# A branch hint for the back edge of the loop over pairs of expert jobs, on TensorE, ScalarE and VectorE

## The reference

```python
def swiglu(h, wg, wu, wd):
    return (jax.nn.silu(h @ wg) * (h @ wu)) @ wd

def moe_swiglu(h, router_w, wg, wu, wd):
    logits = (h @ router_w).astype(jnp.float32)
    top_val, top_idx = lax.top_k(logits, TOP_K)          # TOP_K = 2
    top_w = jax.nn.softmax(top_val, axis=-1)
    gates = jnp.sum(jax.nn.one_hot(top_idx, N_EXPERTS) * top_w[..., None], axis=-2)
    y = jnp.zeros_like(h)
    for e in range(N_EXPERTS):                            # 8 experts, 1024 x 3584 each
        y = y + gates[..., e:e + 1] * swiglu(h, wg[e], wu[e], wd[e])
    return y
```

## Time and profile before

| | us |
|---|---|
| median of 3 runs | 1384.22 (1383.19 to 1384.24) |
| span of the profiled execution | 1382.1 |
| jobs 0 and 1 end, loop entered (TensorE) | 759 |
| back edge (TensorE) | 960 to 967 |
| exit (TensorE) | 1169 to 1173 |

### The profile page before, as it was taken

How to read it: one execution, slowest core, us unless ns; L and a number is a source line. 1 busy time by engine, 2 the same in 40 slices (tenths; PEclk the granted TensorE clock), 3 DMA queues, 4 the chain that set the end, 5 groups by cost and what they waited for, 6 DMA issues and landing times.

```text
span 1382.1 us, 17732 instructions
## 1 busy us (share of the span) xinstructions
PE 1368.8 (99%) x6681; PEld 938.3 (68%) x6681; DVE 808.3 (58%) x1143; ACT 661.5 (48%) x886; POOL 10.3 (1%) x22
## 2 busy tenths in 40 slices
PE   8999999999999999999999999999999999999998
PEld 7887788888898877843434888534888534888532
DVE  5878666554557786631113989423889423989311
ACT  7657646444366575511002787312787302787210
POOL 2000000000000000000000000000000000000000
PEclk9999999999999999999999999999999999999999
DMA  9555446555544576899999999999999999999997
GB/s 354 191 177 184 152 136 231 183 183 184 182 153 155 181 264 269 309 403 429 429 433 427 430 431 428 429 432 428 429 430 423 399 431 427 430 429 430 428 430 295
DMA packets 84242, 454.90 MB, mean 329 GB/s; under 512 B 5624, under 2 KB 7936, under 8 KB 58048
## 3 DMA queue, kind: packets, MB, share of 16 engines
q1 hardware_dynamic: 83232, 452.47, 81.7%
q0 software_dynamic: 752, 1.23, 0.3%
q10 hardware_dynamic: 176, 0.07, 0.0%
HBM read 452.69 MB, written 1.06 MB: 328 GB/s over the span
## 4 chain that ended last, share of the span: by engine, by line
PE 92%; DVE 3%; ACT 3%; DMA 2%; issue 1%; DVEq 0%; ACTq 0%; SPq 0%
PE pA L837 39%; PE pB L837 19%; PE pB L1351 10%; PE pA L1351 8%; PE pA L1415 7%; PE pA L861 2%; DMA first_run<-expert_w_gate_dram 2%; PE pB L861 1%; DVE w_lo L1873 1%; PE pB L1249 1%; ACT w_hi L1514 1%; PE pA L1279 0%; PE pB L1069 0%; ACT early_hi L1514 0%; DMA aqk<-mix_norm_g_dram 0%
## 5 line engine op out<-in xcount | busy, mean ns | idle before, releaser
L1873 DVE TENSOR_TENSOR w_lo<-raw,w_hi 128x1024 fp32r<-128x1024 f32 x128 | 153.1, 1220 | 58.0 <-ACT w_hi L1514 57.6
L1873 DVE TENSOR_TENSOR w_lo<-first_run,w_hi 128x1024 fp32r<-128x1024 f32 x126 | 149.1, 1219 | 30.9 <-ACT w_hi L1514 29.6
L1514 ACT ACTIVATE w_hi<-raw 128x1024 fp32r<-128x1024 f32 x128 | 131.9, 1058 | 56.2 <-PE pB L837 32.2
L1873 DVE TENSOR_TENSOR w_lo<-late,w_hi 128x1024 fp32r<-128x1024 f32 x126 | 150.8, 1222 | 11.9 <-ACT w_hi L1514 3.6
L1514 ACT ACTIVATE w_hi<-first_run 128x1024 fp32r<-128x1024 f32 x126 | 130.9, 1065 | 52.0 <-DMA first_run<-expert_w_gate_dram 26.5
L1514 ACT ACTIVATE w_hi<-late 128x1024 fp32r<-128x1024 f32 x126 | 131.8, 1060 | 30.6 <-PE pA L837 15.1
L1824 ACT ACTIVATE ex_act<-pA 64x512 f32<-64x512 f32 x15 | 8.9, 591 | 242.0 <-PE pA L1351 194.4
L1873 DVE TENSOR_TENSOR early_lo<-raw,early_hi 128x1024 fp32r<-128x1024 f32 x58 | 69.8, 1221 | 34.3 <-ACT early_hi L1514 34.2
L2373 DVE TENSOR_TENSOR x<-pA,x 128x512 f32<-128x512 f32 x28 | 18.8, 688 | 118.2 <-PE pA L1280 116.9
L1351 PE MATMUL pB<-late,x_narrow 128*64 128x512 f32 x272 | 78.0, 592 | 0.0
L837 PE MATMUL pA<-w_hi,hT_hi 128*128 128x512 f32 x192 | 77.1, 402 | 0.0
(11 more groups left out here) (463 smaller groups left out, 2792.8 us busy)
## 6 DMA issues: line engine op xcount, KB each, us to landing
first_run<-expert_w_gate_dram SPq DMA_DIRECT2D x28, 1792.0 KB, 17.7
first_run<-expert_w_up_dram SPq DMA_DIRECT2D x28, 1792.0 KB, 15.3
late<-expert_w_gate_dram SPq DMA_DIRECT2D x28, 1792.0 KB, 15.5
late<-expert_w_up_dram SPq DMA_DIRECT2D x28, 1792.0 KB, 17.4
raw<-w_in_dram SPq DMA_DIRECT2D x43, 1024.0 KB, 5.1
first_run<-expert_w_down_dram SPq DMA_DIRECT2D x21, 2048.0 KB, 15.9
late<-expert_w_down_dram SPq DMA_DIRECT2D x28, 1024.0 KB, 17.6
late<-expert_w_down_dram SPq DMA_DIRECT2D x14, 2048.0 KB, 21.9
```

The lines of the kernel that those rows point to most:

```text
L1514: f(like_raw(m, halves_slot(m)[0]), raw_slot(m), ACT.Copy).then_inc(s["w_hi_done"], 1)
L1873: tt(like_raw(m, lo), raw_slot(m), like_raw(m, hi.bitcast(F32)), ALU.subtract).then_inc(s["w_lo_done"], 1)
```

## The change

`nc.Fori` with one engine stands in the place of the engine's own `Fori`, with the same bounds and the same body. With `hint_back_edge=True` one more instruction is put at the head of the body: a branch prefetch hint that names the compare-and-branch at the body's end and says that it will be taken. It runs in each round. Nothing else in the program differs; SyncE and GpSimd have no such loop.

```diff
@@ -1481,7 +1481,7 @@
             rounds = load_pair_count(pe)
-            with pe.Fori(0, rounds) as i:
+            with nc.Fori(0, rounds, engines=[pe.engine], hint_back_edge=True) as i:
                 job(2 * i + 2, i)
                 narrow_job(i + 2, 2 * i + 3, "wide", "wide", i + 1)
@@ -1842,7 +1842,7 @@
             rounds = load_pair_count(eng)
-            with eng.Fori(0, rounds) as i:
+            with nc.Fori(0, rounds, engines=[eng.engine], hint_back_edge=True) as i:
                 job(2 * i + 2, i)
                 narrow_job(i + 2, 2 * i + 3, "wide", "wide", i + 1)
```

## The result

The changed kernel takes 1390.88 us (median; 1389.90 to 1392.29), the kernel before 1384.22 on the same chip: a ratio of 1.0054, 95% interval 1.0044 to 1.0065, so 0.4% to 0.65% slower. (The ratio is worked out from the single runs; the quotient of the two medians is 1.0048.) Forecast were 1391.8 us, as rival A. The total fits. Its terms are another matter: two of them were wrong and cancelled.

A forecast was written before the change was run, and what follows sets the result against it. TensorE and the loads were taken as full in the expert stage, so only delays to TensorE count. Terms -3.5 + 3.5 + 7.6 = +7.6 on a 1382.1 us span, with 2.1 around it, give 1391.8 us; range 1380.6 to 1397.0.

The forecast's parts named there:

- rival A: The forecast itself: wrong hint at the exit, exposed on ScalarE and VectorE, 1391.8 us (1387 to 1398); chance 0.44.
- Part 1: Loop heads: three hint instructions, run twice each, cost 0; 0.5 us more if nothing covered them.
- Part 2: TensorE's back edge: head's block fetched early removes pause and low clock; between 0 and -3.68, taken as -3.5 us.
- The 1.54 us for the clock: Behind TensorE's back-edge pause: granted clock at 0.50 from 967.2 to 970.6 us costs 1.54 of the 3.68 us.
- Part 3, TensorE: At the loop exit: the wrong hint leaves the next block unfetched, stopping TensorE as at the back edge, +3.5 us.
- Rival B: The wait only moves from TensorE's back edge to its exit, other engines unaffected: 1384.2 us; chance 0.20.
- Part 3, ScalarE and VectorE: Behind the exit: wrong hints stop both engines, 2.2 us of TensorE pause plus low clock each, 3.8 each, +7.6 us.
- The stop S: Behind the exit: ScalarE or VectorE waits some 5.3 us for its code, costing TensorE S - 3.1.
- the cover of 3.1 us: Behind the exit: slack 1.7 us from four slots, plus 1.36 us until the next piece is due, hides that much stop.
- The remark on SiLU in the bounds: Upper bound behind the exit, 15.0 us if no slack is left: at SiLU (L1803) ScalarE has little.
- Rival C: Back edge mended, exit free because prefetch turns to the next block after the branch falls through: 1381.0 us; chance 0.24.
- Rival D: The hint changes nothing, prefetch being purely sequential: 1384.2 us, up to 1384.7; chance 0.12.

The follow-up runs named there:

- slot 0: Against the kernel before, TensorE's loop head at a fetch block's start: ratio 0.9998 without hint, 0.9993 with constant hint, 0.9979 with register hint (not taken in last round).
- 76 or 128: Against the kernel before, TensorE's loop alone with register hint, head at instruction 76 or 128 of its fetch block: 1382.53 us (0.9992) and 1382.49 us (0.9993).
- slot 46: Against the kernel before, TensorE's loop alone with register hint, head at instruction 46 of its fetch block: 1383.67 us, ratio 1.0003.
- VectorE alone: Against the kernel before, the constant hint on VectorE's loop only: 1386.87 us, ratio 1.0028.
- ScalarE alone: Against the kernel before, the constant hint on ScalarE's loop only: 1387.86 us, ratio 1.0030.

## Why the prediction was right, and where it was not

**Part 1**, the hints themselves at 0: right as far as the runs tell. Their rows are 31 to 61 ns, a register move in their place leaves the time as it was, and so do true hints on ScalarE and VectorE.

**Part 2**, TensorE's back edge at -3.5 us: wrong. The step "if the head's block is fetched before the branch needs it" was granted, not weighed. The bound "0 (the fetch comes no earlier)" was named, and it is what happened: branch 6270 ns. With the head at slot 0, 76 or 128 the hint mends it (266 to 510 ns), at slot 46, 2 us behind a boundary, it doesn't. That the changed kernel's branch is also close behind one is the reading that fits (it takes 5944 and 6270 ns in two profiles, no less than without a hint, and the register-move run has the two packets there); the place itself was not measured. The 1.54 us for the clock, of the 3.68, are also not there in every execution. Of ten profiled pauses of 2.0 to 2.7 us, five were followed by a granted clock of 0.50 (before, VectorE alone, ScalarE alone behind the exit, slot 0 with the constant hint, slot 46) and five were not. The kernel before happened to be profiled with one. Its 104 single runs beside the experiments fit that: in 71 the mean granted clock was 0.999 (median 1382.99 us), in 33 it was 0.997 or 0.998 (median 1384.11). So the low clock is worth some 1.1 us in a third of the executions, not 1.54 in all, and the 1384.22 us that the forecast started from looks to be of the longer kind.

**Part 3, TensorE**, +3.5 at the exit: wrong, and it cancelled part 2. The exit took 16.16 us as before. One cause is likely behind both errors, though the changed kernel's own branch was not placed: a hint far behind a boundary acts, and then it mends the back edge and costs at the exit (2.44 us of pause in the run with the constant hint at slot 0); one close behind a boundary does neither. Rival B had this mechanism, and on TensorE it is what a better placed constant hint gives in the profiled execution.

**Part 3, ScalarE and VectorE**, +7.6: right in kind and place, somewhat small. The pauses are 2.86 and 3.13 us, not 2.2 each, and each has its stretch of half clock (1.5). The stop S was taken as 5.3 us. As an estimate: if these fetches too take 3.6 us from the need to the packet, as TensorE's did (branch 960.1, packet 963.7), VectorE stood from 1176.9 to 1182.4, 5.5 us, and ScalarE from 1212.6 to 1217.65, 5.05. Then S was sound, and the term that was mis-sized is the cover of 3.1 us: 5.5 - 2.86 = 2.6 and 5.05 - 3.13 = 1.9. The four slots were taken to be full when the stop comes. Both stops fall where the engine has other work between its pieces, VectorE the two `x` of L2373 and ScalarE the SiLU of L1803, so it had less of a lead than in the steady part; that reading fits the rows and was not tried by itself. The remark on SiLU in the bounds belonged into the sum.

The sum on the span: forecast -3.5 + 3.5 + 7.6 = +7.6, measured in the longest execution +0.4 - 1.6 + 0 + 9.6 = +8.4, and between the medians 6.7. That the total came out is luck in part, since the two wrong terms on TensorE had opposite signs. **Rival C** needed the fetch to turn back at the exit in time. No profile shows it; the two executions of 1379.81 and 1380.10 us with the constant hint at slot 0 have its time. What C gives (1381.0) came with the hint made true, 1380.45. **Rival D**, by which the hint changes nothing, holds on TensorE here and fails on the other two.

The Trainium skill (Runtime: NRT & Kernel Launch, Instruction fetch mechanics) calls prefetch purely sequential. The runs without a hint agree (slot 0 fetches 8 packets in round two although the round fits); with a hint that has its lead they do not, since the head's block is there when the branch is taken (266 ns) and the block behind the exit isn't (2.44 us of pause).

## What to carry to other kernels

A constant hint on a loop's back edge is wrong once, at the exit: weigh what the back edge costs times the rounds against one stop, here some 5 us on each engine of which 2.4 to 3.1 reached TensorE, and leave it off every engine whose loop stays resident, since it has nothing to win there. On the engine whose loop doesn't stay resident, place the head so that the branch stands well behind a block's boundary (5 us mended it here, 2 didn't), and let a register say "not taken" in the last round; of the placings tried, only slot 0 gained clear of noise. Before a term is added for an edit, ask whether the edit can act in time at all; a right total of wrong terms is found only by reading each term off the trace.

## What the runs showed that I had not expected

- A lead of 5 us mends the branch (506 ns), one of 2 us gives nothing (5834 ns), and nothing in between was tried.
- With the hint and the head at slot 0, round two needs 1 or 2 packets of code instead of 8 or 9: without a hint, at the same slot, 8 are fetched.
- With that same constant hint two of eleven executions ran as fast as with a true one.
- The granted clock fell to 0.50 behind five of ten pauses of 2.0 to 2.7 us, and behind all four of 2.8 to 3.6 us. A term for the clock behind a short pause is a chance, not a cost.
